# An opening worked by pieces, three inverse roots on another engine, and an earlier key turn in a two-model transformer kernel

## The reference, cut to what matters

```
mod = silu(c) @ ada_w + ada_b;  sh1, sc1, gt1, sh2, sc2, gt2 = split(mod)
h = rms_norm(x, norm1_gain) * (1 + sc1) + sh1;  z = h @ w_in
q, k of MLA:        rms_norm over each head (q_gain, k_gain)
kw of NSA:          sliding-window keys, normed and rotated
o_a (second stack): rms_norm over each head * (1 - lam_init)
rms_norm(x, g) = x * rsqrt(mean(x * x) + 1e-6) * g
```

## Time and profile before

| | |
|---|---|
| median of 3 runs | 2210.19 us (2209.67 to 2212.11) |
| the profiled execution | 2209.41 us, its span 2207.6 us |
| busy: PE, DVE, ACT, POOL | 97%, 68%, 43%, 54% of the span |
| the chain that ended last | PE 85%, DVE 8%, issue 2%, ACT 2%, DVEq 1%, DMA 1%, POOL 1% |
| mean granted clock of TensorE | 0.996 |
| DMA | 206.78 MB, mean 94 GB/s; 318 GB/s in the first fortieth of the span |

### The profile page before, as it was taken

How to read it: one execution, slowest core, us unless ns; L and a number is a source line. 1 busy time by engine, 2 the same in 40 slices (tenths; PEclk the granted TensorE clock), 3 DMA queues, 4 the chain that set the end, 5 groups by cost and what they waited for, 6 DMA issues and landing times.

```text
span 2207.6 us, 33182 instructions
## 1 busy us (share of the span) xinstructions
PE 2147.7 (97%) x12377; PEld 1839.9 (83%) x12377; DVE 1504.0 (68%) x2242; ACT 954.0 (43%) x1905; POOL 1195.1 (54%) x594
## 2 busy tenths in 40 slices
PE   6999999999999999999999999999999999999997
PEld 4788888877899988897887898888897887889886
DVE  6834777554666692897746776677996727767676
ACT  3264663011556610644743555412545725555312
POOL 4747403776477677745016644577653037544675
PEclk9999999999999999999999999999999999999999
DMA  8422202522133333232002222322221012223221
GB/s 318 156 72 83 68 30 94 189 80 96 58 116 115 113 140 134 77 115 77 1 13 84 96 96 95 115 96 85 106 85 69 1 35 82 88 103 115 96 96 57
DMA packets 32776, 206.78 MB, mean 94 GB/s; under 512 B 4080, under 2 KB 4336, under 8 KB 11632
## 3 DMA queue, kind: packets, MB, share of 16 engines
q1 hardware_dynamic: 32192, 200.27, 25.2%
q10 hardware_dynamic: 432, 4.46, 0.5%
HBM read 202.61 MB, written 2.10 MB: 93 GB/s over the span
## 4 chain that ended last, share of the span: by engine, by line
PE 85%; DVE 8%; issue 2%; ACT 2%; DVEq 1%; DMA 1%; POOL 1%; POOLq 0%; SPq 0%; ACTq 0%
PE PS L1130 18%; PE PS L1132 18%; PE PS L1131 18%; PE PS L1626 4%; PE PS L1615 4%; PE PS L1385 3%; PE PS L1387 3%; PE PS L1386 3%; PE PS L1461 2%; PE PS L1463 2%; PE PS L1462 2%; PE PS L1640 2%; PE PS L1260 1%; PE PS L1263 1%; PE PS L1262 1%
## 5 line engine op out<-in xcount | busy, mean ns | idle before, releaser
L668 POOL TENSOR_TENSOR w_hi<-raw,zero_c 128x512 fp32r<-128x512 f32 (+1 forms) x135 | 281.6, 2104 | 545.0 <-PE PS L1132 543.7
L672 POOL TENSOR_TENSOR w_lo<-raw,w_hi 128x512 fp32r<-128x512 f32 (+1 forms) x135 | 365.0, 2722 | 5.8
L1130 PE MATMUL PS<-b_hi,w_hi 128*128 128x512 f32 x512 | 203.1, 397 | 1.0 <-POOL w_lo L891 1.0
L1132 PE MATMUL PS<-b_hi,w_lo 128*128 128x512 f32 x512 | 203.0, 396 | 0.0
L1131 PE MATMUL PS<-b_lo,w_hi 128*128 128x512 f32 x512 | 203.0, 396 | 0.0
L3376 DVE TENSOR_TENSOR b_lo<-a_all,b_hi 128x512 fp32r<-128x512 f32 x44 | 162.6, 3734 | 49.3 <-ACT b_hi L2511 49.3
L1130 PE MATMUL PS<-f_hi,w_hi 128*128 128x512 f32 x448 | 177.6, 396 | 0.7 <-DVE f_lo L2668 0.7
L1132 PE MATMUL PS<-f_hi,w_lo 128*128 128x512 f32 x448 | 177.6, 396 | 0.0
L1131 PE MATMUL PS<-f_lo,w_hi 128*128 128x512 f32 x448 | 177.6, 396 | 0.0
L691 POOL TENSOR_TENSOR w_lo<-raw,w_hi 128x512 fp32r<-128x512 f32 x48 | 71.1, 1481 | 92.7 <-ACT w_hi L2503 92.7
L1130 PEld LDWEIGHTS PS<-b_hi,w_hi 128*128 128x128 f32 x512 | 96.4, 188 | 24.7 <-POOL w_lo L891 1.2
(11 more groups left out here) (600 smaller groups left out, 6890.1 us busy)
## 6 DMA issues: line engine op xcount, KB each, us to landing
raw<-slabs_dram SPq DMA_DIRECT2D x161, 1024.0 KB, 4.8
aux<-ada_dram SPq DMA_DIRECT2D x18, 512.0 KB, 5.5
ada_first<-ada_dram SPq DMA_DIRECT2D x11, 512.0 KB, 14.2
cmpw<-cmpw_dram ACTq DMA_DIRECT2D x2, 2048.0 KB, 12.0
ada_late<-ada_dram SPq DMA_DIRECT2D x8, 512.0 KB, 3.4
ada_last<-ada_dram SPq DMA_DIRECT2D x8, 512.0 KB, 6.1
xT<-xT_dram SPq DMA_DIRECT2D x1, 2048.0 KB, 9.2
out_dram<-t SPq DMA_DIRECT2D x4, 512.0 KB, 3.2
```

The source lines that it names most:

```text
L668: high = nc.gpsimd.tensor_tensor(w_hi[:, slot, c], raw[:, slot, c], zero[:, 0:c.stop - c.start], ALU.add)
L672: low = nc.gpsimd.tensor_tensor(w_lo[:, slot, c], raw[:, slot, c], w_hi[:, slot, c].bitcast(f32), ALU.subtract)
L1130: nc.tensor.matmul(out, a_hi_, b_hi_, start=start, stop=False)
L1132: return nc.tensor.matmul(out, a_lo_, b_hi_, start=False, stop=stop)
```

## The change

Three things are done at once.

The opening: SP loads xT in two halves with consts between them; cols counts to the first rows' semaphore. ScalarE waits for a half before it squares. VectorE adds the squares by pairs, so that TensorE's mean takes four matmuls; 20 unread matmuls follow in place of 16. The reciprocal goes straight to inv_rms in SBUF, and GpSimd multiplies each block by it (t1). ScalarE makes h_hi from t1 with scale and shift in one instruction, then the shift minus h_hi in PS bank 4 or 5, and VectorE makes h_lo as t1 times scale plus that. Only row 0 of adaLN is done ahead of the reciprocal. The high pieces of slabs 2, 3 and 0 are copied by ScalarE, the low ones are subtracted by GpSimd, in one order with the multiplications (first_slabs); the second pair's first slab is taken by pieces too.

The inverse roots: MLA's and the differential heads' are computed by GpSimd, with a pow and one Newton step (inverse_root). The Sqrt on ScalarE and the reciprocal on VectorE go.

The sliding keys: turned after token tile 0 in place of tile 1, and copied out before the first take_kv.

```diff
             sp.dma_start(crow[:], c_d.partition_broadcast(P)).then_inc(crow_loaded, 16)
-            sp.dma_start(xT[:], xT_d).then_inc(x_loaded, 16)
-            for dst, src in ((consts[:], consts_d), (cols[:], cols_d)):
-                sp.dma_start(dst, src).then_inc(const_loaded, 16)
+            for i in (0, 1):
+                sp.dma_start(xT[:, 4 * i:4 * i + 4, :], xT_d[:, 4 * i:4 * i + 4, :]).then_inc(x_loaded[i], 16)
+                if i == 0:
+                    sp.dma_start(consts[:], consts_d).then_inc(const_loaded, 16)
+            sp.dma_start(cols[:], cols_d).then_inc(ada_first_loaded[0], 16)
...
+            def first_slabs():
+                def normed(k):
+                    nc.gpsimd.tensor_tensor(t1[:, k, :], xT[:, k, :], inv_rms[:], ALU.mult).then_inc(part_ready, 1)
+
+                pool.wait_ge(inv_kept, 1)
+                normed(0)
+                for k in range(KD + 4):
+                    if k + 1 < KD:
+                        normed(k + 1)
+                    n, c = k // 4 % 2, slice(PIECE * (k % 4), PIECE * (k % 4) + PIECE)
+                    if k >= KD:
+                        pool.wait_ge(slab_used, 1)
+                    pool.wait_ge(piece_hi, k + 1)
+                    nc.gpsimd.tensor_tensor(w_lo[:, n, c], raw[:, n, c], w_hi[:, n, c].bitcast(f32),
                                             ALU.subtract).then_inc(piece_split, 1)
+                    if k % 4 == 3:
+                        pool.drain().then_inc(hi_done, 1)
+                        pool.drain().then_inc(slab_split, 1)
...
+            def inverse_root(v, d, y, e):
+
+                nc.gpsimd.tensor_scalar(v, v, 1.0 / d, EPS, ALU.mult, ALU.add)
+                pool.drain()
+                nc.gpsimd.tensor_tensor(y, v, power_c.to_broadcast(list(v.shape)), ALU.pow)
+                pool.drain()
+                nc.gpsimd.tensor_tensor(e, y, y, ALU.mult)
+                pool.drain()
+                nc.gpsimd.tensor_tensor(e, e, v, ALU.mult)
+                pool.drain()
+                nc.gpsimd.tensor_scalar(e, e, -0.5, 1.5, ALU.mult, ALU.add)
+                pool.drain()
+                nc.gpsimd.tensor_tensor(v, e, y, ALU.mult)
+                pool.drain()
+
             def mla_heads():
 
-                pool.wait_ge(mla_inv, 1)
+                pool.wait_ge(mla_sum, 3)
+                inverse_root(stats[:, 144:208], MLA_QK, stats[:, 0:64], stats[:, 64:128])
...
+                for layer, ct in enumerate(COUNTS):
+                    if n == ct.up:
+                        for k in (at, at + 1):
+                            split(k % 2, k, k // 2)
+                        at += 2
+                        pool.wait_ge(diff_sum, layer + 1)
+                        inverse_root(stats[:, 0:16], HD, stats[:, 16:32], stats[:, 32:48])
+                        pool.drain().then_inc(diff_root, 1)
...
-            chunk(4, between=during_q)
+            chunk(4, ready=lambda k: pe.wait_ge(piece_split, KD + k + 1), between=during_q)
...
-                if tt == 1:
+                if tt == 0:
                     pe.wait_ge(kw_ready, 1)
                     pe.wait_ge(q_taken_dve, 1)
                     nsa_turn(REP + 1, 3)
...
+            def piece_high(k):
+                n, c = k // 4, slice(PIECE * (k % 4), PIECE * (k % 4) + PIECE)
+                act.wait_ge(slab_loaded[n % 2], 16 * (n // 2) + 16)
+                A(w_hi[:, n % 2, c], raw[:, n % 2, c], ACT.Copy).then_inc(piece_hi, 1)
+
+            for k in range(KD):
                 first_mod(k)
                 act.wait_ge(part_ready, k + 1)
                 act.drain()
-                A(h_hi[:, k, :], PS[:, 5, :], ACT.Identity, bias=mod[:, k:k + 1]).then_inc(part_hi, 1)
-                if k == 2:
-                    A(inv_rms[:], PS[:, 4, :], ACT.Copy).then_inc(inv_kept, 1)
+                A(h_hi[:, k, :], t1[:, k, :], ACT.Identity, scale=mod[:, KD + k:KD + k + 1], bias=mod[:, k:k + 1])
+                act.drain()
+                if k >= 2:
+                    act.wait_ge(part_low, k - 1)
+                A(PS[:, 4 + k % 2, :], h_hi[:, k, :].bitcast(f32), ACT.Identity, scale=-1.0, bias=mod[:, k:k + 1]
+                  ).then_inc(part_hi, 1)
+                piece_high(k)
+            act.wait_ge(slab_used, 1)
+            for k in range(KD, KD + 4):
+                piece_high(k)
...
             act.wait_ge(c_summed, 1)
             q_squares(0)
+            keys_high(1, 3)
             take_kv(0)
             act.wait_ge(q_taken_dve, 2)
             q_squares(1)
-            keys_high(1, 3)
...
-                if step == 8:
-                    act.wait_ge(mla_sum, 3)
-                    A(stats[:, 144:208], stats[:, 144:208], ACT.Sqrt, scale=1.0 / MLA_QK, bias=eps_c
-                      ).then_inc(mla_root, 1)
...
+                V.scalar_tensor_tensor(out=h_lo[:, k, :], in0=t1[:, k, :], scalar=sc1[:, k:k + 1],
+                                       in1=PS[:, 4 + k % 2, :], op0=ALU.mult, op1=ALU.add).then_inc(part_low, 1)
...
+            first_shift(0)
+            first_scale(0)
             dve.wait_ge(root_ready, 1)
...
+            V.reciprocal(inv_rms[:], PS[:, 1, :]).then_inc(inv_kept, 1)
+            ahead = {0: (1, 2), 1: (3,), 3: (4,), 4: (5,), 5: (6,), 6: (7,)}
+            for k in range(KD):
+                for row_ in ahead.get(k, ()):
+                    first_shift(row_)
+                    first_scale(row_)
                 first_low(k)
...
-                if step == 10:
-                    dve.wait_ge(mla_root, 1)
-                    V.reciprocal(stats[:, 144:208], stats[:, 144:208]).then_inc(mla_inv, 1)
```

More of the change, by code:

```diff
@@ L412, in build @@
         lam_c = small[:, 2:3]
-        const_loaded, crow_loaded, x_loaded = sem("const_loaded"), sem("crow_loaded"), sem("x_loaded")
+        power_c = small[:, 46:47]
+        const_loaded, crow_loaded, x_loaded = sem("const_loaded"), sem("crow_loaded"), [sem(f"x_loaded{i}") for i in (0, 1)]
         rest_loaded = sem("rest_loaded")
         ada_first_loaded = [sem(f"ada_first_loaded{q}") for q in range(KD)]
-        mod_summed, mod_ready, inv_kept = sem("mod_summed"), sem("mod_ready"), sem("inv_kept")
+        mod_summed, inv_kept = sem("mod_summed"), sem("inv_kept")
         piece_hi, piece_split = sem("piece_hi"), sem("piece_split")
@@ L846, in _ @@
             n_pieces = (N_IN + N_TAIL + N_QB + N_KVB) // 2
-            split_first(0)
-            split_first(1)
-            with pool.Fori(1, N_IN // 2) as i:
+            first_slabs()
+            split(1, 3, 1, piece=PIECE)
+            with pool.Fori(2, N_IN // 2) as i:
                 for s in (0, 1):
@@ L861, in run @@
                     n0 += 1
-                with pool.Fori(n0 // 2, n1 // 2) as i:
-                    for s in (0, 1):
-                        split(s, 2 * i + s, i)
+                if n1 // 2 > n0 // 2:
+                    with pool.Fori(n0 // 2, n1 // 2) as i:
+                        for s in (0, 1):
+                            split(s, 2 * i + s, i)
                 if n1 % 2:
@@ L1134, in norm @@
             def norm(t, residual=True, warm=16):
-                ks = (3, 5, 6, 7) if residual else range(KD)
+                ks = (3, 5, 6, 7) if residual else (1, 3, 5, 7)
                 for k in ks:
-                    if residual and k < 6:
+                    if not residual or k < 6:
                         pe.wait_ge(pair_ready, at_.pairs + 1)
@@ L1143, in norm @@
                         pe.wait_ge(sq_ready, KD * at_.norms + k + 1)
-                    last = nc.tensor.matmul(PS[:, 0, :], mean_w, t[:, k, :], start=not residual and k == 0,
+                    last = nc.tensor.matmul(PS[:, 0, :], mean_w, t[:, k, :], start=not residual and k == ks[0],
                                             stop=k == ks[-1])
@@ L1189, in chunk @@
                 for s in (0, 1):
-                    pe.wait_ge(slab_split, at_.slab + 1)
-                    slab_tokens(at_.slab % 2, h_hi, h_lo, 4 * s, 4, n, bank0, 1, s == 0, s == 1, ready,
+                    if not ready or s:
+                        pe.wait_ge(slab_split, at_.slab + 1)
+                    slab_tokens(at_.slab % 2, h_hi, h_lo, 4 * s, 4, n, bank0, 1, s == 0, s == 1, None if s else ready,
                                 banks_ready if s == 0 else None,
@@ L2961, in _ @@
-            dve.wait_ge(x_loaded, 16)
-            dve.wait_ge(const_loaded, 16 * 2)
+                V.scalar_tensor_tensor(out=h_lo[:, k, :], in0=t1[:, k, :], scalar=sc1[:, k:k + 1],
+                                       in1=PS[:, 4 + k % 2, :], op0=ALU.mult, op1=ALU.add).then_inc(part_low, 1)
+            for k in range(0, KD, 2):
+                dve.wait_ge(sq_ready, k + 2)
+                V.tensor_tensor(t1[:, k + 1, :], t1[:, k, :], t1[:, k + 1, :], ALU.add).then_inc(pair_ready, 1)
+            dve.wait_ge(ada_first_loaded[0], 48)
@@ L2963, in _ @@
```

(21 more changed lines are left out.)

45 lines of the change are left out of this document (8 added, 37 removed).

## The result

The changed kernel is slower: 2215.7 us (median of 10 runs, 2213.0 to 2217.9) against 2211.1 (2208.2 to 2212.1), a ratio of 1.0024 with a 95% interval of 1.0016 to 1.0031. The forecast was 2197.0. The profiled execution took 2213.90 us, its span is 2212.1; before they were 2209.41 and 2207.6, so the two traces differ by 4.5 us, and they can be laid beside each other. The table takes the same instruction of TensorE in both.

What follows compares the result with a forecast made beforehand. It took TensorE as busy nearly all the span and the opening as bound by VectorE. Gains of 5.7, 1.5, 5.4 and 0.6 sum to 13.2: 2209.4 becomes 2196.2, with the median's 0.8 2197.0; range 2192 to 2204.

Steps and rivals of the forecast that it cites:

- ScalarE did not become its pace: Rival in the opening: ScalarE at 3.5 us a block sets the pace, 3.3 of the gain go, 2200.3; chance 0.15.
- A: Opening: earlier mean and cheaper blocks start the second pair's second slab at 64.3 against 70.0; 5.7 us gained.
- B: Kv projection: sliding keys turned one tile sooner remove TensorE's wait before token tile 3; 1.5 us gained.
- C: First attention: Sqrt and two table loads go, GpSimd's inverse root takes 3.8, 0.4 too late; 5.4 us gained.
- all three signs of being wrong: Opening piece or slab wait above 1 us, GpSimd pow above 3.2, or TensorE waiting for kv_x at the k turn.
- the load in A: Opening: SP's slab load starts near 48.1, cmpw is issued 0.9 behind it, and the slab lands at 55.
- a rival had it at another place: Clock stays low in the first attention or falls after the opening's 1.6 stand: 3.0 us back, 2200; chance 0.10.
- D: Two later inverse roots: moving them to GpSimd gains 0.3 us each, 0.6 together.
- The one on the other side: Rival: pow computed element by element, kernel slower from 13 us for 64 columns, 2220 at 20; chance 0.06.
- A's own 7.8: Opening: the slab load's full duration when cmpw goes out beside it, which would leave 4.8 us gained.
- The third rival: GpSimd's first pow call costs extra and delays the k turn: 2201 at 4 us extra; chance 0.12.
- the forecast's own range: Whole kernel: 2193, with all upper ends and the clock's full 3.4 us, to 2199; the forecast had chance 0.55.

Runs made afterwards that it cites:

- Experiment 1: Changed kernel with ScalarE issuing the two cmpw loads behind its two staging copies; 2209.0 us, 0.9990 of the kernel before.
- experiment 6: Changed kernel with all inverse roots back on ScalarE and VectorE and the cmpw loads issued behind ScalarE's two Sin; 2203.3 us.
- Experiment 4: Changed kernel with eleven unread matmuls ahead of the turns of the second pair's first slab; 2212.9 us.
- Experiments 2 and 7: 2: changed kernel, first attention's pow made a multiplication, 2205.2 us; 7: kernel before, only the first attention's inverse root moved to GpSimd, 2216.2 us.
- experiment 9: Changed kernel with cmpw behind ScalarE's two Sin, and the first attention's head turns and adaLN rows due nine steps later; 2196.7 us.
- experiment 3: Changed kernel with the first attention's inverse root back on ScalarE and VectorE; 2212.6 us.

## Why the prediction was wrong

**What held.** The opening ran as worked out up to the turns: reciprocal 17.79 to 21.15 (18.3 to 21.7), first product 26.90 (27.5), no gap on TensorE of more than half a microsecond from there to the turns, which came at 60.93, 1.0 sooner than the 61.9 of the sum (0.3 of it is a slip: 43.4 and 2.7 give 46.1, not 46.4). ScalarE did not become its pace. The keys gave 1.7 (1.5). Without the table loads the attention gained 6.5 us up to 244 (5.8), clock included: it stayed at 1.00 from 75 to 245 us. Of that, 0.8 went again when VectorE's small operations ran beside GpSimd. So the gains of A, B and C were there before two steps lost more than they brought; all three signs of being wrong that the prediction names at its end came with them.

**The first failed step is the load in A:** "cmpw is now issued by ScalarE near 49.0, 0.9 behind. I take landing at 55." The issue was put at the place in time at which ScalarE would have finished the instructions ahead of it. The trace shows 44.34, while ScalarE still had four pieces to convert, so cmpw stood 2.4 us ahead of the slab and not 0.9 behind it, and the slab landed at 57.95. (The row at 52.01 of the kernel before could have told: that issue came at the start of the conversion ahead of it, not at its end.) With GpSimd's 9.5 instead of 9.2 the slab started at 67.55, not 64.3: 3.3 us. Another 0.3 is the slab's start before, 69.72 and not 70.0, and 2.8 are the clock behind the stand: together 6.3, from 5.7 gained to 0.6 lost. The sum had no term for a clock that falls behind a *new* stand, though the earlier trace rows showed one behind an old stand; a rival had it at another place. Experiment 1 gives the opening's 7 us back by moving that issue alone, and 1 us of them goes again at the next slab; experiment 6, with all roots back as well, keeps them. Experiment 4 separates stand and clock.

**The second failed step is the price of the pow in C.** It was taken at 1.5 and bounded at 3.2, "ten multiplies"; it costs 10.55, as much as 36 of the 0.29. Ten was a number without a row behind it, so it was no bound. VectorE's reciprocal was the nearest row, but it is another operation on another engine. What followed from the price was right: by "Each us beyond 3.4 of inverse root is paid at the k turn", an inverse root of 12.9 us (221.95 to 234.83) makes the k turn 9.5 late; it came at 260.15, where 257.47 less the 6.74 gained by then gives 250.73: 9.4 late. The q turn, of which the sum does not speak, had already stood 3.6 of that. Behind it 4.5 us at half clock, 2.25, were again in no sum. Experiments 2 and 7 show the pow as the cause, with and without the rest of the change, and experiment 9 that it is the pow together with the time at which its readers ask.

**D** was to gain 0.3 at each place and lost 0.1. The margin was right, 4.5 us from the sums to VectorE's question (1108.88 to 1113.4). The same term failed as in C: the pow of 16 columns takes 2.91, so the whole root is ready only when VectorE has waited 0.35, more than there was to gain.

**The rivals.** The one on the other side had the right price law: the pow's time grows with its columns, 2.91 us for 16 and 10.55 for 64, 0.16 a column. It was given 0.06, and by itself it would not have reached the other side. Its formula is counted from the 13.6 us that the rest gains, so from 2196.6; with q = 10.55 it gives 2196.6 + 9.45 + 2 x 0.14 = 2206.3, and with the 2.25 of the clock behind the turns 2208.6. Experiment 1, which loses only 1 us of the opening's gain, measured 2209.0. The 6.3 of load and clock in the opening make that 2214.9; measured were 2215.7. No rival had a load later than A's own 7.8, and the slow pow stood alone: for a loss on both together there was no chance at all. The third rival, a first call that costs extra, did not happen: the pow of 64 columns starts 0.15 us after the operation ahead of it, and the two later calls of 16 columns take 2.905 and 2.912 us, so that its 10.55, less than four times that, has no room for some 6 us. The six microseconds of the Trainium skill, GPSIMD Engine Reference, Instruction dispatch, stand nowhere in these rows.

**Slips of its sums,** beside the one above. The ends that A to D name add up to 2195 and 2201, not to the 2193 and 2199 of the forecast's own range. The time left to GpSimd's root is 250.2 - 25.2 - 221.4 = 3.6, not 3.4. Twice the drain of 1.38 that C quotes is 2.8, not 2.5. None of them moves the result.

**A number met for another kernel.** Experiment 9 measured 2196.7, next to the 2197.0 that was forecast. Its trace has the terms, too: 7.35 in the opening (5.7), 1.7 at the keys (1.5), 5.7 in the attention (5.4). But two things had to be moved for it that the prediction took to be in place, so it does not make the prediction right.

## What to carry to other kernels

An operation that no row shows has no upper bound in multiples of one that is shown: ask instead from which price on its reader waits, and either give the reader that time (nine steps here, worth 11 us in the attention) or measure the operation first. When a stretch is made to start sooner, look at every load that is issued in it, with the time at which its *queue* can issue it, and put bulk that is read late behind what is read next. A sum in which TensorE gets a new stand, like those of 3.6 to 5.8 us here, should carry a second term for the clock behind it; in the opening it was 1.4 to 2.8 us in three traces, at the turns 2.25 of the 11.7 us lost up to 265 us (0.7 of which are back by 293).

## What the runs showed of the hardware that was not expected

GpSimd's pow costs about 0.16 us for every column of 128 partitions, 10.55 us for 64, beside 0.29 for a multiplication. While GpSimd works through a slab, small operations of VectorE that take 0.16 to 0.22 us alone take 0.9 to 1.25 (experiment 6; in the gaps of GpSimd's work, at 51.94 and 70.57, they take 0.21 and 0.16). ScalarE's queue issued a DMA 2.9 us before the ScalarE instructions that stand ahead of it in the program had ended (44.34 against 47.25). A stand of 4.7 us on TensorE was followed by 5.8 us at 0.50 of the clock, one of 4.8 in experiment 3 by about 3, and one filled with unread matmuls by none; after the opening's new stand of 1.2 us the clock stayed at 1.00.

And TensorE's pace is not the same in all executions even at the same granted clock. The same stretch of the changed kernel and of experiment 6 (busy time by stretch, as above):

```profile
700.00:760.00 60.00, 60.00 (x513) 60.00 (x513) 36.55 (x58) 35.27 (x68) 40.46 (x30) 1.00 0.32 113
```

```profile
700.00:760.00 60.00, 60.00 (x508) 60.00 (x507) 35.64 (x54) 35.20 (x67) 38.14 (x27) 1.00 0.31 106
```

513 and 508 matmuls in 60 us, both without a gap: 1% over some 150 us, here between 610 and 760. At the same instructions experiment 6 falls back by 1.7 us in this stretch and experiment 4 by 3.4, which is why the readings above are taken from offsets within a stage, and the times from medians. What makes it was not tried.
